# Two neighbouring weight units of the expert products in one 1024 KB transfer

## What is computed

```
u = jnp.take(expert_down, ec, axis=0)
hdn = jax.nn.gelu(jnp.einsum('ted,td->te', u, xc))
vsel = jnp.take(expert_up, ec, axis=0)
return jnp.einsum('te,ted->td', gc * hdn, vsel)
```

## Time and profile before

| | |
|---|---|
| median of 3 runs | 2796.92 us |
| span of the profiled execution | 2794.3 us |
| runs above that span | 2.6 us |
| TensorE matmul busy | 2778.8 us, 99% |
| TensorE weight load busy | 2385.7 us, 85% |
| VectorE busy | 1821.7 us, 65% |
| ScalarE busy | 1410.8 us, 50% |
| GpSimd busy | 745.9 us, 27% |
| DMA | 559.01 MB, mean 200 GB/s |

### The profile page before, as it was taken

How to read it: one execution, slowest core, us unless ns; L and a number is a source line. 1 busy time by engine, 2 the same in 40 slices (tenths; PEclk the granted TensorE clock), 3 DMA queues, 4 the chain that set the end, 5 groups by cost and what they waited for, 6 DMA issues and landing times.

```text
span 2794.3 us, 38959 instructions
## 1 busy us (share of the span) xinstructions
PE 2778.8 (99%) x14898; PEld 2385.7 (85%) x14898; DVE 1821.7 (65%) x2878; ACT 1410.8 (50%) x2001; POOL 745.9 (27%) x411
## 2 busy tenths in 40 slices
PE   9999999999999999999999999999999999999998
PEld 7888888888888888888888888888888888999886
DVE  6567666877777655555555555566777876555555
ACT  5455654455555544454444444546655555444454
POOL 0012200388888888810000000001201111000000
PEclk9999999999999999999999999999999999999999
DMA  7654478877777777777677777766655546666664
GB/s 274 211 166 130 153 253 306 261 189 190 189 190 190 190 190 189 190 219 222 213 221 222 212 240 222 234 211 188 185 183 156 160 153 193 189 189 189 188 198 156
DMA packets 199017, 559.01 MB, mean 200 GB/s; under 512 B 53344, under 2 KB 69872, under 8 KB 195888
## 3 DMA queue, kind: packets, MB, share of 16 engines
q1 hardware_dynamic: 161744, 556.04, 64.4%
q0 software_dynamic: 36944, 0.41, 2.6%
q10 hardware_dynamic: 144, 0.07, 0.0%
HBM read 535.32 MB, written 21.12 MB: 199 GB/s over the span
## 4 chain that ended last, share of the span: by engine, by line
PE 96%; DVE 2%; ACT 1%; issue 0%; DMA 0%; SPq 0%; POOL 0%; DVEq 0%; ACTq 0%
PE bank L542 95%; PE bank L554 1%; DVE wlo L953 1%; ACT whi L1717 1%; DMA VV<-in_xT 0%; ACT aX L1717 0%; DVE QKb L956 0%; DVE AT L1218 0%; ACT L1717 0%; DVE lbs L1227 0%; ACT scr L1717 0%; DVE HB L956 0%; ACT DD L1717 0%; DVE tmpc L956 0%; DVE aX L998 0%
## 5 line engine op out<-in xcount | busy, mean ns | idle before, releaser
L953 DVE TENSOR_TENSOR wlo<-raw,whi 128x1024 fp32r<-128x1024 f32 (+1 forms) x965 | 1193.0, 1237 | 850.6 <-ACT whi L1717 847.8
L1717 ACT ACTIVATE whi<-raw 128x1024 fp32r<-128x1024 f32 (+1 forms) x967 | 1017.3, 1054 | 999.8 <-PE bank L542 986.5
L542 PE MATMUL bank<-aX,whi 128*128 128x512 f32 (+1 forms) x4000 | 967.4, 391 | 0.0
L542 PE MATMUL bank<-whi,aX 128*128 128x512 f32 x2944 | 910.4, 390 | 0.7 <-DVE aX L956 0.4
L542 PEld LDWEIGHTS bank<-aX,whi 128*128 128x128 f32 (+1 forms) x4000 | 728.0, 188 | 142.3 <-issue 3.7
L1677 POOL DMA_INDIRECT gate_scratch<-gate,place x256 | 589.6, 2303 | 249.2 <-DMA gate_scratch<-HB 170.7
L542 PEld LDWEIGHTS bank<-whi,aX 128*128 128x128 f32 x2944 | 552.6, 188 | 118.1 <-DVE aX L956 1.9
L542 PE MATMUL bank<-wlo,aX 128*128 128x512 f32 x1472 | 571.7, 389 | 1.4 <-DVE wlo L953 1.4
L542 PEld LDWEIGHTS bank<-aX,wlo 128*128 128x128 f32 (+1 forms) x3984 | 513.1, 191 | 21.2 <-issue 0.5
L542 PE MATMUL bank<-aX,wlo 128*128 128x256 f32 (+1 forms) x3984 | 529.2, 283 | 0.1
L542 PEld LDWEIGHTS bank<-wlo,aX 128*128 128x128 f32 x1472 | 276.3, 188 | 59.4 <-DVE wlo L953 2.6
(11 more groups left out here) (233 smaller groups left out, 1907.5 us busy)
## 6 DMA issues: line engine op xcount, KB each, us to landing
raw<-in_w_down SPq DMA_DIRECT2D x256, 512.0 KB
raw<-in_w_up SPq DMA_DIRECT2D x256, 512.0 KB
raw<-in_w_in SPq DMA_DIRECT2D x176, 512.0 KB
raw<-in_w_out SPq DMA_DIRECT2D x32, 512.0 KB
gate_scratch<-HB SPq DMA_DIRECT2D x16, 1024.0 KB, 7.5
raw<-in_w_pq SPq DMA_DIRECT2D x32, 512.0 KB
raw<-in_w_o SPq DMA_DIRECT2D x32, 512.0 KB
raw<-in_w_pg SPq DMA_DIRECT2D x32, 512.0 KB
```

What stands on the lines that cost most here:

```text
L542: return e.matmul(o, lhsT, rhs, start=start, stop=stop, skip_group_check=True)
L953: e.tensor_tensor(wlo[:, s, 0:n], raw[:, r, 0:n], whi[:, s, 0:n].bitcast(F32), ALU.subtract).then_inc(s_lo, 1)
L1717: return e.activation(o, i, f, **k)
```

## The change

For the 128 groups of the down product and the first 120 of the up product, SP issues one transfer for both units of a group. The host lays out each group as 128 rows of 8 KB. The transfer fills two neighbouring slots of `raw`. For that all slots are shifted by 3 (`SLOT`), so that every pair begins at slot 0 or 2. A pair waits for both slots: for u being its first unit, SP waits for `s_lo` of unit u - 3, where the first unit alone waited for unit u - 4. Both splits of a pair wait for the whole pair (`LANDED`). The last 16 up units, which are ordered by half, come one at a time, with rows of 4 KB at a step of 8 KB. Nothing else moves: TensorE, VectorE, ScalarE and GpSimd have the same instructions in the same order.

```diff
+    rows_down = I["w_down"]
+    I["w_down"] = rows_down.rearrange("i p (u c) -> i u p c", u=2)
...
+    WIDE = {G["down", i].first: rows_down[i].rearrange("p (u c) -> p u c", u=2) for i in range(128)}
...
-    plan.src += [I["w_up"][i, half] for i, half in UPS]
+    plan.src += [I["w_up"][i, :, half * UNIT:half * UNIT + UNIT] for i, half in UPS]
...
+    WIDE |= {UP0 + 2 * i: I["w_up"][i].rearrange("p (u c) -> p u c", u=2) for i in range(120)}
...
+    SLOT = [(u + 3) % NRAW for u in range(NU)]
+    LANDED, landings = {}, [0] * NRAW
+    for u in range(NU):
+        if u - 1 in WIDE:
+            LANDED[u] = LANDED[u - 1]
+        else:
+            landings[SLOT[u]] += 16
+            LANDED[u] = s_raw[SLOT[u]], landings[SLOT[u]]
...
         def load(u):
-            if u >= NU:
+            if u >= NU or u - 1 in WIDE:
+                return
+            r = SLOT[u]
+            if u in WIDE:
+                w.wait_ge(s_lo, u - NRAW + 2)
+                e.dma_start(raw[:, r:r + 2, :], WIDE[u]).then_inc(LANDED[u][0], 16)
                 return
             if u >= NRAW:
                 w.wait_ge(s_lo, u - NRAW + 1)
-            e.dma_start(raw[:, u % NRAW, 0:plan.src[u].shape[-1]], plan.src[u]).then_inc(s_raw[u % NRAW], 16)
+            e.dma_start(raw[:, r, 0:plan.src[u].shape[-1]], plan.src[u]).then_inc(LANDED[u][0], 16)
```

More of the change, by code:

```diff
@@ L949, in split @@
             if u < NU:
-                n, r, s = plan.src[u].shape[-1], u % NRAW, u % NSPL
-                w.wait_ge(s_raw[r], 16 * (u // NRAW + 1))
+                n, r, s = plan.src[u].shape[-1], SLOT[u], u % NSPL
+                w.wait_ge(*LANDED[u])
                 w.wait_ge(s_hi, u + 1)
@@ L1935, in _ @@
                 u = kt // 2
-                w.wait_ge(s_raw[u], 16)
-                act(whi[:, u, 0:512], raw[:, u, 0:512], ACT.Copy).then_inc(s_h0, 1)
-                act(whi[:, u, 512:1024], raw[:, u, 512:1024], ACT.Copy).then_inc(s_hi, 1)
+                w.wait_ge(*LANDED[u])
+                act(whi[:, u, 0:512], raw[:, SLOT[u], 0:512], ACT.Copy).then_inc(s_h0, 1)
+                act(whi[:, u, 512:1024], raw[:, SLOT[u], 512:1024], ACT.Copy).then_inc(s_hi, 1)
             if kt in (7, 11):
@@ L2176, in arrays @@
     a["w_down"] = np.ascontiguousarray(
-        g["peer_down"][0].reshape(128, 128, 2, 8, 128).transpose(0, 2, 4, 3, 1)).reshape(128, 2, 128, 1024)
+        g["peer_down"][0].reshape(128, 128, 2, 8, 128).transpose(0, 4, 2, 3, 1)).reshape(128, 128, 2048)
     a["w_up"] = np.ascontiguousarray(
-        g["peer_up"][0].reshape(128, 128, 2, 1024).transpose(0, 2, 1, 3))
+        g["peer_up"][0].reshape(128, 128, 2048))
     a["keys"] = np.ascontiguousarray(g["peer_sub_keys"][0].reshape(16, 128, 128).transpose(2, 0, 1)).reshape(128, 2048)
```

## The result

The changed kernel takes 2805.86 us (median of 6 runs, 2804.55 to 2807.05), the one before, measured again beside it, 2796.77 us. The ratio is 1.0032 with a 95% interval of 1.0020 to 1.0043: slower by 9.1 us. The profiled span is 2803.8 us against 2794.3. The time lies in the range; the single time forecast, 2801.7 us, took the clock to hold, and it did not. The 2.6 us that I took as the distance between span and runs was too much: each of the six runs is 1.9 to 2.0 us above its own span, and so is every run of the kernel before that was measured beside the experiments. The 2.6 had set a median of three runs against the span of a fast one.

The account below looks back on a forecast made before the run. TensorE, busy 2778.8 of 2794.3 us, was taken as the bound. All terms cost 0 but a 4.8 us stall at the first gate load: 2796.92 + 4.8 = 2801.7 us, range 2797.5 to 2810.

Parts of the forecast that it names:

- What bounds the kernel, the steady products: Both expert products: TensorE bounds them, up product 2.721 us a unit; a pair lands in 4.7 us, cost 0.
- the 5.4 and 5.9 us that the timelines left: Time from a pair's issue to ScalarE wanting its even unit: 5.4 us in up product, 5.9 us in down product.
- The bound of 6.1 us: Fastest traced 1024 KB load landing; at this, pairs late throughout the up product cost 42 us, 2844 us; rival's chance 0.12.
- The first gate load: Before up unit 4: load issued 5.0 us late behind pair 6, 7, TensorE stands still 4.8 us (3.5 to 6.2).
- this rival: Clock falls to half in the stall before up unit 4: 2803.8 us, or 2805.8 if low twice as long; chance 0.27.
- The row of the program's end: After the last matmul, ended at 2783.04, the clock stayed 1.00 for 4.4 us, then went to 0.50.
- the nearer case: After the stall, low clock lasts as long as the idleness that brought it, 4.4 us: 2.1 us lost, 2803.8 us.
- The time of 2805.8 us: Fallen-clock rival, chance 0.27 in all, with the low clock after the stall lasting twice as long as the idleness.
- the loop of a ring that holds two pairs: Up product: four units take landing time L + 5.47 us against 10.88; past L = 5.4 TensorE waits; rival's chance 0.12.
- The zero fill and the scatters: Last zero fill behind down pair 8, 9: scatters start up to 4.6 us later, `g0` still 1.7 us early, cost 0.
- No gain: TensorE waits for no weight load in the steady products; larger rows gain under 1 us at the start; faster, chance 0.03.

Follow-up runs that it names:

- the kernel with the short stall: Changed kernel, first gate load issued ahead of the pair of up units 6, 7, but after waiting for up unit 3's low part: 2801.74 us, ratio 1.0017.
- The last experiment: Changed kernel with first gate load ahead of the pair 6, 7, and from up unit 16 every pair waiting one unit more: 3025.17 and 3033.03 us.

## Why the prediction came out as it did

**What bounds the kernel, the steady products.** Right. Both products keep their pace, 2.721 us an up unit, for 198 units. A pair lands after 4.9 us, inside the 5.4 and 5.9 us that the timelines left. Even so ScalarE's waits name the pair 13 times in these units, for 1.3 to 2.3 us, which I had not expected; TensorE's lead covered them. The bound of 6.1 us, read from a load that shared the queue, had nothing to do with it; the Trainium skill (DMA: Bandwidth & Descriptors, Bandwidth) and its 6.15 us for 1 MB, which the page gives for transfers issued from GpSimd, is above what this trace shows for a pair issued from SP.

**The first gate load.** The mechanism, the place and most of the size were right: issue 5.2 us later (5.0 forecast), landing at about 1241.9 (1241.2), stall 5.8 us (4.8 forecast, 3.5 to 6.2 as its bounds). The term that was too small is the bytes ahead of it. I let 512 KB more cost 1.3 us. From 5.5 to 7.25 us they cost 1.75, more than the rate of a deep queue gives. That is 0.45 of the 1.0 us missing. Of the rest 0.2 is the later issue, 0.2 that the up product started early, and the others lie between landing and restart.

**The clock.** This is the step that failed. I gave the forecast a stall at full clock, 0.45, and this rival 0.27. The row of the program's end, a fall 4.4 us after the last matmul, had been read as a threshold: "it decides once TensorE idles somewhat beyond 4 us". In the changed kernel TensorE idled from 1243.34 - 5.46 = 1237.88, and the clock fell at 1241.98, 4.1 us into the stall. In the kernel with the short stall it came after 2.25 us of idleness and 1.5 us of work. One row says that idleness lowers the clock; it does not say how little is enough. The last experiment says more: 14 of 17 stops of 2.1 to 3.1 us cost the clock, and none of 76 between 1.0 and 1.9 us. The price of 0.47 us for each microsecond at the lower level was right (427 against 227 ns a matmul). The length of the low stretch was not: 6.8 us, 5.5 of them with TensorE at work, where I had 4.4 as the nearer case; 2.6 us were lost and not 2.1. The Trainium skill's rule (TensorE: Matmul & The Clock Gate, Part 1), that only sustained work gives the clock back, fits: the low clock outlasted the stall in both kernels.

**The time of 2805.8 us.** The rival named it for a low clock twice as long as the idleness, and 2805.86 was measured. That is luck: it is made of a stall 1.0 us longer, a clock that cost 2.6 us and not the 4.1 of that case, and 1.2 us at the end of the product that no case had.

**The last groups of the up product.** I left this out. I had priced the loop of a ring that holds two pairs, L + 5.47 us a round of four units against 10.88, and looked at it in the steady part alone. In groups 96 to 119 the lower bounds of the recurrence are computed on the side (`lower_bounds` on VectorE, `Exp` and `Ln` on ScalarE, and a `Sqrt` behind them), with three table loads of 1.28 us between ScalarE's splits. The chain's rows show it: from one pair's issue to the next-but-one's 1813.99 - 1803.64 = 10.35 us (4.92 + 5.43, the formula) in a round without a table load, but 1803.64 - 1791.72 = 11.92 and 1825.88 - 1813.99 = 11.89 us with one. Each such round is 1 us beyond TensorE's 10.88, and TensorE's lead is 1.4 us. It costs 1.2 to 1.5 us in four profiles and about 0.8 in that of the same wait, and single loads there remove it. That it is the table loads and not VectorE's small operations beside them was not tried by itself. But the round from 1780.90 to 1791.72 has such operations and no table load, and took 10.82 us, still within TensorE's 10.88.

**The zero fill and the scatters.** Harmless, as forecast, but not as worked out: the last fill was issued at 525.79 and the scatters began 5.6 us later (4.6 forecast), and then ended 156 us earlier, as told below.

**No gain.** Right: nothing was faster. TensorE waited for no weight load before.

## What to carry to other kernels

- Merging two loads does not touch TensorE's pace while a pair lands within the slack. But everything that stands behind it in the same queue inherits its later wait and its bytes. Look for the first one-off load after each change of stage.
- A loop's slack must be read at the place where the other engines have the most extra work, not in the steady part.
- Once TensorE stands still for about 2 us or more, add the clock to the bill: here stops of 2.1 to 5.5 us mostly cost it, stops up to 2.0 us never did.

## What was not expected of the hardware

**The clock can fall after the work is back.** After 2.25 us of idleness, TensorE ran at full clock for 1.5 us and then at half for 3.4 us. In the kernel with the pair one unit later this was the rule: 10 of the 14 falls came after TensorE was back at work.

**The scatters on GpSimd.** The median of the 256 indirect transfers was 2.47 us in the kernel before and 1.55 us in every kernel with pairs in the down product, with rows of 8 KB or of 4 KB (count, ns shortest/median/longest, first and last start; before, then after):

```profile
L1677 POOL DMA_INDIRECT gate_scratch<-gate,place x256: 1541/2466/2516, 528.9 to 1194.5; - x128
```

```profile
L1694 POOL DMA_INDIRECT gate_scratch<-gate,place x256: 1541/1550/2600, 534.5 to 1038.4; - x128
```

Nothing waited for them, so it changed no time here. GpSimd's stream of work and its data are the same; what differs is when the weights arrive. Before, a scatter and its gap mostly took as long as a down unit, 2.8 us, and from 699 to 712 us each one started 0.15 to 0.18 us behind a `wlo` of VectorE; now most take 1.86. Whether the two engines hold each other up there was not tried. The cause stays open.
